# The last output chunk of a two-layer decoder trunk, finished one token tile at a time

## What is computed

```python
def rmsnorm(x, g):
    xf = x.astype(jnp.float32)
    y = xf * lax.rsqrt(jnp.mean(xf * xf, axis=-1, keepdims=True) + NORM_EPS)
    return (y * g.astype(jnp.float32)).astype(x.dtype)

# end of the odd layer, then the trunk's end; o is 256 x 2048
y = (o * jax.nn.silu(gate)) @ w_out          # w_out 2048 x 2048
x = x + y
return rmsnorm(x, final_norm)
```

## Time and profile before

| what | value |
|---|---|
| time, median of 3 runs | 841.35 us |
| lowest and highest of the 3 | 841.31 us, 842.04 us |
| time of the profiled execution | 841.62 us |
| its span in the profile | 839.8 us |
| granted TensorE clock, mean over the span | 0.996 of full speed |
| PE busy | 815.3 us, 97% of the span |
| DVE, ACT, POOL busy | 445.8, 405.7, 121.1 us |
| bytes moved by DMA | 139.04 MB, of which 2.10 MB written |

### The profile page before, as it was taken

The page is one execution under the profiler, slowest core; times in us unless marked ns, Lnnn a source line. Parts: engine busy times, 40 slices in busy tenths (PEclk is TensorE's granted clock), DMA queues, the critical chain, the costliest instruction groups (busy, mean ns, idle before and its releaser), DMA issues.

```text
span 839.8 us, 11569 instructions
## 1 busy us (share of the span) xinstructions
PE 815.3 (97%) x4025; PEld 688.4 (82%) x4025; DVE 445.8 (53%) x589; ACT 405.7 (48%) x573; POOL 121.1 (14%) x244
## 2 busy tenths in 40 slices
PE   5999999999999999999999999999999999999994
PEld 4878888888888888887888888888888998888883
DVE  3565666565444454546445544344545655664552
ACT  4664344445444554564445635344554454554451
POOL 5400221200001010030000100020013113100230
PEclk9999999999999999999999999999999999999998
DMA  8855564656665656543567566566534245355502
GB/s 271 306 151 155 152 175 131 179 163 167 184 181 170 177 159 189 175 151 115 189 198 204 172 198 178 152 196 171 167 116 128 93 131 201 104 173 175 197 29 100
DMA packets 76649, 139.04 MB, mean 166 GB/s; under 512 B 8840, under 2 KB 13104, under 8 KB 76480
## 3 DMA queue, kind: packets, MB, share of 16 engines
q1 hardware_dynamic: 76320, 137.96, 54.5%
q10 hardware_dynamic: 288, 0.52, 0.2%
HBM read 136.37 MB, written 2.10 MB: 165 GB/s over the span
## 4 chain that ended last, share of the span: by engine, by line
PE 92%; DVE 3%; ACT 1%; issue 1%; DMA 1%; POOL 1%; ACTq 0%; SPq 0%; POOLq 0%; DVEq 0%
PE ps L1114 27%; PE ps L1116 27%; PE ps L1115 26%; PE ps L1239 1%; PE ps L1135 1%; PE ps L1460 1%; PE ps L1461 1%; PE ps L1196 1%; PE ps L1417 1%; DMA raw<-in_w_in_even 1%; DVE w_lo L1031 1%; PE ps L1426 0%; PE ps L1435 0%; PE ps L1165 0%; PE ps L1164 0%
## 5 line engine op out<-in xcount | busy, mean ns | idle before, releaser
L797 DVE TENSOR_TENSOR w_lo<-raw,w_hi 128x1024 fp32r<-128x1024 f32 (+1 forms) x224 | 281.0, 1255 | 298.6 <-ACT w_hi L520 293.3
L1114 PE MATMUL ps<-w_hi,a_hi 128*128 128x512 f32 (+1 forms) x1024 | 401.6, 392 | 3.9 <-DVE a_lo L822 3.4
L1116 PE MATMUL ps<-w_hi,a_lo 128*128 128x512 f32 (+1 forms) x1024 | 396.6, 387 | 0.0
L1115 PE MATMUL ps<-w_lo,a_hi 128*128 128x512 f32 (+1 forms) x1024 | 396.2, 387 | 0.0
L520 ACT ACTIVATE w_hi<-raw 128x1024 fp32r<-128x1024 f32 (+1 forms) x220 | 232.5, 1057 | 301.1 <-PE ps L1116 300.3
L1114 PEld LDWEIGHTS ps<-w_hi,a_hi 128*128 128x128 f32 x1024 | 192.9, 188 | 41.7 <-DVE a_lo L822 3.6
L1116 PEld LDWEIGHTS ps<-w_hi,a_lo 128*128 128x128 f32 x1024 | 192.8, 188 | 38.2
L1115 PEld LDWEIGHTS ps<-w_lo,a_hi 128*128 128x128 f32 x1024 | 193.0, 188 | 36.2
L1031 DVE TENSOR_TENSOR w_lo<-raw,w_hi 128x1024 fp32r<-128x1024 f32 (+1 forms) x32 | 34.8, 1104 | 21.1 <-ACT w_hi L736 20.9
L473 POOL TENSOR_TENSOR work<-even,cos_ 128x128 f32<-128x128 f32 x16 | 11.8, 739 | 146.4 <-DVE even L809 146.4
L452 POOL TENSOR_TENSOR xs<-xs,work 128x512 f32<-128x512 f32 x7 | 12.9, 1837 | 132.7 <-ACT work L532 132.7
(11 more groups left out here) (188 smaller groups left out, 595.0 us busy)
## 6 DMA issues: line engine op xcount, KB each, us to landing
raw<-in_w_in_even SPq DMA_DIRECT2D x112, 512.0 KB, 3.7
raw<-in_w_in_odd SPq DMA_DIRECT2D x48, 512.0 KB, 3.6
raw<-in_w_out_even SPq DMA_DIRECT2D x32, 512.0 KB, 3.7
raw<-in_w_out_odd SPq DMA_DIRECT2D x32, 512.0 KB, 3.9
raw<-in_w_kv_up SPq DMA_DIRECT2D x16, 512.0 KB, 3.7
raw<-in_w_q_up SPq DMA_DIRECT2D x16, 384.0 KB, 3.3
xs<-in_x SPq DMA_DIRECT2D x6, 256.0 KB, 6.6
even<-in_final_norm SPq DMA_DIRECT2D x1, 1024.0 KB, 6.7
```

Source lines behind the costliest of these rows:

```text
L797: v.tensor_tensor(w_lo[:, s % RING, 0:w], raw[:, s % RAW, 0:w], w_hi[:, s % RING, 0:w].bitcast(F32), ALU.subtract).then_inc(lo_ready, 1)
L1114: m.matmul(acc, a_hi[:, k, tok], hi, start=first, stop=False)
L1115: m.matmul(acc, a_hi[:, k, tok], lo, start=False, stop=False)
L1116: ins = m.matmul(acc, a_lo[:, k, tok], hi, start=False, stop=last)
```

## The change

The last chunk gets a function of its own on TensorE. The first four pieces are used as before, for both token tiles. The last four are used for token tile 0 first and then, from the same four slots, for token tile 1, with a signal (`tail_done`) after each token tile. The other engines finish token tile 0 completely and then token tile 1. For each, DVE adds the residual in two halves of 256 columns, and ACT squares each half. POOL sums the squares of chunks 0 to 2 for both token tiles ahead, as soon as they are there. DVE adds the sums of the two halves with one small instruction each (`scalar_tensor_tensor` on 128x1), POOL takes the power for one token tile, and the scaling of a token tile is done by DVE (three pieces of 512 columns) and ACT (one piece of 512). There are four stores of 128x512 for each token tile: SP issues three and ACT's own queue the fourth.

```diff
@@ sync
-            for n, cols in enumerate((slice(2 * CW, 3 * CW), slice(0, 2 * CW), slice(3 * CW, 4 * CW))):
-                for t in range(T):
-                    sp.wait_ge(fin_d if t else fin_a, n + 1)
-                    sp.dma_start(out_d[t][:, cols], final_pieces(t)[n]).then_inc(out_written, 16)
-            sp.wait_ge(out_written, 16 * 3 * T)
+            for t in range(T):
+                sp.wait_ge(fin_d, 3 * t + 1)
+                sp.dma_start(out_d[t][:, 0:CW], xs[:, t, 0:CW]).then_inc(out_written, 16)
+                sp.wait_ge(fin_d, 3 * t + 2)
+                sp.dma_start(out_d[t][:, CW:2 * CW], xs[:, t, CW:2 * CW]).then_inc(out_written, 16)
+                sp.wait_ge(fin_d, 3 * t + 3)
+                sp.dma_start(out_d[t][:, TAIL:], stg[1][:, t, :]).then_inc(out_written, 16)
+            sp.wait_ge(out_written, 16 * 4 * T)
@@ gpsimd
-            stream_sums(32, 8)
-            inverse_root(8, 10, D, None)
+            pool.wait_ge(sq_ready, 28)
+            v = ssum[:, 32:40].rearrange("p (t s) -> p t s", t=T)
+            step(g.tensor_tensor(v[:, :, 0], v[:, :, 0], v[:, :, 1], ALU.add))
+            step(g.tensor_tensor(ssum[:, 8:10], v[:, :, 0], v[:, :, 2], ALU.add))
+            g.tensor_scalar(ssum[:, 10:12], ssum[:, 8:10], 1.0 / D, EPS, ALU.mult, ALU.add).then_inc(pre_ready, 1)
+            for t in range(T):
+                pool.wait_ge(stat_seq, 2 * t + 2)
+                g.tensor_tensor(rstd[:, 8 + t:9 + t], ssum[:, 10 + t:11 + t], half[:, t:t + 1], ALU.pow).then_inc(stat_ready, 1)
@@ scalar
             for t in range(T):
-                act.wait_ge(evac_d, C_OUT1 + 4 + t)
-                squares(xs[:, t, 3 * CW:], ssum[:, 35 + 4 * t:36 + 4 * t], sq_junk)
-
-            act.wait_ge(rstd_ready, 5)
-            for n, out_part in enumerate(final_pieces(0)):
-                if n == 2:
-                    act.wait_ge(last_gained, 1)
+                for i in range(2):
+                    act.wait_ge(tail_added, 2 * t + i + 1)
+                    half_junk = work[:, 3072 + HW * (2 * t + i):3072 + HW * (2 * t + i) + HW]
+                    a.activation(half_junk, xs[:, t, tail_half(i)], ACT.Square,
+                                 accum_out=ssum[:, 12 + 2 * t + i:13 + 2 * t + i]).then_inc(sq_ready, 1)
+                act.wait_ge(stat_ready, t + 1)
                 act.wait_ge(res_gained, 2 * 3)
-                a.activation(out_part, out_part, ACT.Copy, scale=rstd[:, 8:9]).then_inc(fin_a, 1)
+                part = xs[:, t, 2 * CW:3 * CW]
+                a.activation(part, part, ACT.Copy, scale=rstd[:, 8 + t:9 + t]).then_inc(fin_a, 1)
+                act.wait_ge(fin_a, t + 1)
+                act.dma_start(out_d[t][:, 2 * CW:3 * CW], part).then_inc(out_written, 16)
@@ vector
             for t in range(T):
-                dve.wait_ge(evac_d, C_OUT1 + 4 + t)
-                v.tensor_tensor(stg[1][:, t, :], xs[:, t, 3 * CW:], fin_g[:, 3 * CW:], ALU.mult).then_inc(last_gained, 1)
-            dve.wait_ge(rstd_ready, 5)
-            dve.wait_ge(res_gained, 2 * 3)
-            for n, out_part in enumerate(final_pieces(1)):
-                if n == 2:
-                    dve.wait_ge(last_gained, 2)
-                v.tensor_scalar(out_part, out_part, rstd[:, 9:10], None, ALU.mult).then_inc(fin_d, 1)
+                dve.wait_ge(tail_done, t + 1)
+                for i in range(2):
+                    dst = xs[:, t, tail_half(i)]
+                    v.tensor_tensor(dst, dst, ps[:, 2 + t, HW * i:HW * i + HW], ALU.add).then_inc(tail_added, 1)
+                dve.wait_ge(tail_added, 2 * t + 2)
+                v.tensor_tensor(stg[1][:, t, :], xs[:, t, TAIL:], fin_g[:, TAIL:], ALU.mult).then_inc(last_gained, 1)
+                dve.wait_ge(pre_ready, 1)
+                for i in range(2):
+                    dve.wait_ge(sq_ready, 28 + 2 * t + i + 1)
+                    if i:
+                        dve.wait_ge(stat_seq, 2 * t + 1)
+                    v.scalar_tensor_tensor(out=ssum[:, 10 + t:11 + t], in0=ssum[:, 12 + 2 * t + i:13 + 2 * t + i], scalar=1.0 / D,
+                                           in1=ssum[:, 10 + t:11 + t], op0=ALU.mult, op1=ALU.add).then_inc(stat_seq, 1)
+                dve.wait_ge(stat_ready, t + 1)
+                dve.wait_ge(res_gained, 2 * 3)
+                dve.wait_ge(last_gained, t + 1)
+                for part in (xs[:, t, 0:CW], xs[:, t, CW:2 * CW], stg[1][:, t, :]):
+                    v.tensor_scalar(part, part, rstd[:, 8 + t:9 + t], None, ALU.mult).then_inc(fin_d, 1)
@@ tensor
+            def last_chunk(n0, c):
+
+                project(n0, c, 1, tiles=NP // 2, close=False)
+                for t in range(T):
+                    acc = ps[:, 2 + t, :]
+                    tok = slice(t * P, t * P + P)
+                    for j in range(NP // 2, NP):
+                        s = j % RING
+                        pe.wait_ge(lo_ready, n0 + (j + 1))
+                        for kk in range(PK):
+                            k = PK * j + kk
+                            hi, lo = w_hi[:, s, kk * CW:kk * CW + CW], w_lo[:, s, kk * CW:kk * CW + CW]
+                            m.matmul(acc, a_hi[:, k, tok], hi, start=False, stop=False)
+                            m.matmul(acc, a_hi[:, k, tok], lo, start=False, stop=False)
+                            ins = m.matmul(acc, a_lo[:, k, tok], hi, start=False, stop=k == KT - 1)
+                    ins.then_inc(tail_done, 1)
-            out_projection(B_OUT1, C_OUT1, (last_pair, None, None, None))
+            out_projection(B_OUT1, C_OUT1, (last_pair, None, None))
+            last_chunk(NP * (B_OUT1 + 3), C_OUT1 + 3)
```

More of the change, by code:

```diff
@@ L227, in build @@
         rope_seq, q_roped, qkt_done, qt_ready, kt_ready = (sem(n) for n in ("rope_seq", "q_roped", "qkt_done", "qt_ready", "kt_ready"))
+        tail_done, tail_added, pre_ready, stat_seq, stat_ready = (sem(n) for n in ("tail_done", "tail_added", "pre_ready", "stat_seq", "stat_ready"))
         sc_done, sc_max, nmx_ready, p_ready, rinv_ready, my_done, my_ready = (
@@ L230, in build, with tail_half @@
         res_gained, last_gained, fin_a, fin_d, out_written = (sem(n) for n in ("res_gained", "last_gained", "fin_a", "fin_d", "out_written"))
-        def final_pieces(t):
-            return xs[:, t, 2 * CW:3 * CW], xs[:, t, 0:2 * CW], stg[1][:, t, :]
+        HW = CW // 2
+        TAIL = 3 * CW
+        def tail_half(i):
+            return slice(TAIL + HW * i, TAIL + HW * i + HW)
         def halves(v, L):
@@ L968, in outputs @@
                     ahead(b + n, pieces=4 if last else 8, between=plan)
+                    if last:
+                        return
                     dve.wait_ge(piece_used, pieces_through(c + n, part))
-                    for t in range(T) if last else (1,):
-                        dst = xs[:, t, CW * n:CW * n + CW]
-                        v.tensor_tensor(dst, dst, ps[:, 2 * (n % 2) + t, :], ALU.add).then_inc(evac_d, 1)
+                    dst = xs[:, 1, CW * n:CW * n + CW]
+                    v.tensor_tensor(dst, dst, ps[:, 2 * (n % 2) + 1, :], ALU.add).then_inc(evac_d, 1)
             y_prep, x1_prep = prep(steps_from(U_PREPY)), prep(steps_from(U_PREP1), 16)
@@ L1093, in _, with project @@
             m = nc.tensor
-            def project(n0, c, par, wait=True, tiles=NP, k0=0, s0=0, n=CW, before=None):
+            def project(n0, c, par, wait=True, tiles=NP, k0=0, s0=0, n=CW, before=None, close=True):
                 if wait:
@@ L1109, in project @@
                         hi, lo = w_hi[:, s, kk * n:kk * n + n], w_lo[:, s, kk * n:kk * n + n]
-                        first, last = j == 0 and kk == 0, j == tiles - 1 and kk == PK - 1
+                        first, last = j == 0 and kk == 0, close and j == tiles - 1 and kk == PK - 1
                         for t in range(T):
```

## The result

| | before | changed |
|---|---|---|
| time, median of 5 runs | 841.83 us | 837.16 us |
| lowest and highest | 841.31, 842.14 | 836.65, 837.69 |
| profiled execution: time, span | 841.62, 839.8 us | 837.69, 835.8 us |
| last matmul's start | 827.54 | 827.79 |
| last matmul's start to the end of the span | 12.26 us | 8.01 us |

The ratio is 0.9947, 95% interval 0.9936 to 0.9958: faster by 0.53%. (It is taken over all runs; the two medians alone give 0.9945.) The forecast was 837.4, range 836.5 to 838.9. Against the 841.35 from which the prediction started, the saving is 4.19 us where 3.99 were forecast. By the interval it lies between 3.5 and 5.4 us.

The account below looks back on a forecast made before the run. Matmuls bound the kernel up to the last one, then a relay plus store bytes bound by the DMA engines. Savings of 1.26 + 0.23 + 2.50 = 3.99 us take 841.35 to 837.4, range 836.5 to 838.9.

Parts of the forecast that it names:

- The matmuls: Last chunk on TensorE: the new order gains nothing there, and its end stays at 827.97.
- Long runs in a bank: Last chunk's second half: 24 matmuls staying in one bank were taken to cost 0.
- the last piece in time: Last chunk: DVE's conversion done at 820.49, wanted by TensorE at 820.97, a margin of 0.48 us.
- Token tile 0, hidden: Kernel's end: token tile 0's work and 1.05 MB run under token tile 1's matmuls and relay, with 5.44 us of cover.
- Token tile 1, the relay: After the last matmul, add to power: `rstd` used at 830.64 against 831.90, 1.26 us saved.
- The small steps: In the relay: POOL's three steps (0.86 us) leave the path, paid by 0.5 on DVE.
- The bytes: Last stores: 1.05 MB instead of 2.10 remain, 2.83 us at 371 GB/s against 5.33, 2.50 us saved.
- Two queues at nothing: Last stores: issues of 0.45 us stay ahead of 0.7 us of bytes a store, so two queues or one makes no difference.
- The dear power: Rival, POOL in the relay: the power on one column costs 2.09 us, 1.5 more on the path, giving 838.9; chance 0.10.
- The wait for the last piece: Rival, last chunk: TensorE waits 0.1 to 0.4 us for the last piece, giving 837.5 to 837.8; chance 0.08.
- the bytes that don't get shorter: Rival, stores: token tile 0's drain only with the others, the 2.50 is lost, giving 839.9; chance 0.05.
- the bank: Rival, last chunk: long runs in one bank lose matmul overlap, costing 7.8 us, net 3.8 slower, 845.2; chance 0.02.

## Why the prediction was right

- *The matmuls.* Their end at 827.97 was forecast as unchanged. It came 0.25 later, as did the whole last chunk (its first matmul starts at 806.26 instead of 806.01), so that lies ahead of the change. It is luck that the span came out at 835.8, exactly as forecast: the last matmul came 0.25 late, and the end stretch was 0.26 shorter than the sum had it. Long runs in a bank at 0, and the last piece in time by 0.48: both shown.
- *Token tile 0, hidden.* Forecast: adds at 822.53, `rstd` used at 825.1, DVE free at 826.5, first bytes at 826.6. Measured, with the 0.25 of the drift: 822.88, 825.37, 826.65, 826.77. (The first add came 0.53 us after token tile 0's last matmul started at 822.35, where 0.43 was taken; the room had space for it.) That it is hidden is shown by the run without its stores and by the run with one product more; that the room is needed, by the old order (3.11).
- *Token tile 1, the relay.* Forecast 1.26 saved, measured 1.44. The 0.18 is the sum of small terms that I had taken a little too high. The largest is 0.11 between the starts of the gain product and of the first small step: 0.61 was measured where I had 0.72, because an instruction on DVE starts 0.08 before its neighbour ends. The power was 0.56 (0.60 taken). The small step was 0.156 (0.17 taken; the lower bound of 0.06 had no row of such an operation behind it). One time in this stretch was added up wrongly: the second square, from 828.98 with 0.38 and 0.18, is there at 829.54 and not at 829.45, so by its own terms ACT and not DVE would have been the later. It had no effect on the result: the second sum was read at 829.58, before the first small step began at 829.62.
- *The small steps.* Taking POOL's three steps of 0.86 out and paying 0.5 on DVE was to save 0.36 net, and finishing token tile 1 alone the other 0.90 of the 1.26. The run with the sums back in the relay splits the measured 1.44: it uses `rstd` 3.37 us after the last matmul's start, where the kernel before has 4.36 and the changed one 2.92, so 0.99 and 0.45. (It has no halves, so the split is good to about 0.1.) Against one small step, without halves, taking them out is worth 0.56. The second small step is the price of the halves, and costs more than they bring.
- *The bytes.* 2.50 forecast, 2.57 measured (2.60 by packets), and 2.78 when undone. I had read 371 GB/s as the rate of 2 KB rows, from a window that holds the start of the burst. It was 383. Two queues at nothing: shown.
- *The rivals.* The dear power (2.09) didn't come. Its row is hardly the price of four columns: 1.21 of it lie beside VectorE's conversion, which the prediction had not looked at. If that is the wait it looks like, this rival and the upper end of the range (838.9) rested on something that nothing in the new end brings back, since VectorE itself waits there for the power. The wait for the last piece, the bytes that don't get shorter and the bank fell, each by a run or a row of its own.
- POOL's 1.17 and 2.27 agree with the rule of the lock in the Trainium skill (SBUF — State Buffer, "SBUF: two separate sides"). The Trainium skill's rule of at least 1 MiB in one DMA (DMA: Bandwidth & Descriptors, "Rules for kernel authors") was not needed here: 256 KB stores that follow one another ran at 383 GB/s, and 392 with a 512 KB one among them.

## What to carry to other kernels

When a kernel ends with work per group of rows and a burst of output, read the end as a relay plus bytes, and finish the groups one after the other on the engine that feeds them: each group's bytes then flow under the next one's matmuls and relay. The order alone and the split end alone were worth 0.00 and 1.14 us here, and together 4.25, so a part of such a change tried alone says little of the whole. Compare ends by the stretch from the last matmul, not by the span, when the differences are of a few tenths of a us.

## What the runs showed of the hardware

- An instruction of VectorE with two SBUF inputs that waits for POOL's to end went before POOL's next one, whether that was a small step or a product: 2.31 us for the conversion each time, and about 1.0 us more for POOL's instruction.
- POOL's wait stands in its instruction's own duration: 1.17 us instead of 0.20, 2.27 instead of 1.28, and perhaps the power of 2.09 us, of which 1.21 lie beside a conversion.
- The power on POOL: 0.56 us for one column, in the changed kernel and in every run that has it, 0.71 for two in the kernel before.
- From a store's issue to its first packet 0.82 to 0.87 us, and from the last packet to the end of the span 0.81 to 0.83 us in twelve profiles and 1.16 in one, with 1 or 2 MB and on one or two queues.
